# RWKV chunks: crossed halves, four array quarters for the second products, four heads as one group

## The reference, cut to what matters

```python
def step(state, inp):
    r_t, w_t, k_t, v_t, kk_t, a_t = inp
    sa = jnp.einsum('bhvk,bhk->bhv', state, -kk_t)
    state = (state * w_t[:, :, None, :] + sa[..., None] * (kk_t * a_t)[:, :, None, :]
             + v_t[..., None] * k_t[:, :, None, :])
    return state, jnp.einsum('bhvk,bhk->bhv', state, r_t)
```

## Time and profile before

| | |
|---|---|
| median of 3 runs | 3188.74 us (3184.62 to 3189.36) |
| profiled execution | 3188.14 us, span 3186.3 us |
| busy over the span | PE 3017.8 us (95%), PEld 2578.0 (81%), DVE 2129.0 (67%), ACT 1069.1 (34%), POOL 957.2 (30%) |
| mean granted TensorE clock | 0.985 of full |

### The profile page before, as it was taken

One profiled execution on the slowest core, in us unless ns is written; L12 is line 12 of the kernel. 1 busy time (PEld: TensorE's weight loads), 2 busy tenths in 40 slices (PEclk: granted clock), 3 DMA queues, 4 the chain that ended last, 5 costly groups with the idle time before them and its releaser, 6 DMA issues. The chain is left out here.

```text
span 3186.3 us, 44443 instructions
## 1 busy us (share of the span) xinstructions
PE 3017.8 (95%) x18182; PEld 2578.0 (81%) x18182; DVE 2129.0 (67%) x2634; ACT 1069.1 (34%) x1555; POOL 957.2 (30%) x656
## 2 busy tenths in 40 slices
PE   7999998999999999999998999898999999999997
PEld 7997888999888898887876786666777886888875
DVE  4535675445466646898836655777957757877798
ACT  2012433201133323322012221666415453344534
POOL 2320000333100013553322432111333443554575
PEclk9999999999999999999999999999999999999998
DMA  3111000111100002434242004321532543555543
GB/s 143 47 40 37 23 1 7 68 60 41 55 9 22 1 27 66 157 113 123 96 162 83 3 3 129 93 67 64 205 139 89 181 157 127 160 166 175 159 152 122
DMA packets 114818, 284.38 MB, mean 89 GB/s; under 512 B 15238, under 2 KB 20998, under 8 KB 114600
## 3 DMA queue, kind: packets, MB, share of 16 engines
q1 hardware_dynamic: 111304, 276.83, 26.9%
q10 hardware_dynamic: 3312, 4.72, 0.4%
HBM read 239.47 MB, written 41.44 MB: 88 GB/s over the span
## 5 line engine op out<-in xcount | busy, mean ns | idle before, releaser
L4082 PE MATMUL psum<-x,w_hi 128*128 128x512 f32 x2016 | 626.0, 392 | 8.3 <-DVE x L4053 3.2
L199 POOL CAST w_hi<-w_raw 128x1024 fp32r<-128x1024 f32 x98 | 109.0, 1112 | 1556.6 <-PE psum L212 953.6
L4082 PEld LDWEIGHTS psum<-x,w_hi 128*128 128x128 f32 x2016 | 378.5, 188 | 92.7 <-issue 7.0
L4082 PE MATMUL psum<-x,w_lo 128*128 128x512 f32 x1008 | 393.1, 390 | 0.0
L1061 PE MATMUL psum<-h,w_hi 128*128 128x512 f32 x1024 | 332.2, 406 | 18.8 <-PEq L126 8.5
L3967 POOL TENSOR_TENSOR w_lo<-w_sum,w_hi 128x512 fp32r<-128x512 f32 x180 | 250.6, 1399 | 330.9 <-ACT w_hi L3961 330.8
L203 POOL TENSOR_TENSOR w_lo<-w_raw,w_hi 128x1024 fp32r<-128x1024 f32 x98 | 258.7, 2640 | 14.9 <-DVE y L1876 7.2
L1061 PEld LDWEIGHTS psum<-h,w_hi 128*128 128x128 f32 x1024 | 190.8, 192 | 68.9 <-issue 21.6
L4082 PEld LDWEIGHTS psum<-x,w_lo 128*128 128x128 f32 x1008 | 189.8, 188 | 40.1
L212 PE MATMUL psum<-hn_hi,w_hi 128*128 128x348 f32 x864 | 188.9, 327 | 17.1 <-DVE hn_lo L409 15.7
L1061 PE MATMUL psum<-h,w_lo 128*128 128x512 f32 x512 | 203.1, 397 | 0.0
(11 more groups left out here) (503 smaller groups left out, 6557.3 us busy)
## 6 DMA issues: line engine op xcount, KB each, us to landing
w_raw<-in_w_mlp SPq DMA_DIRECT2D x169, 256.0 KB, 2.9
norm_factor<-in_w_mlp SPq DMA_DIRECT2D x87, 256.0 KB, 2.8
w_raw<-in_w_mlp SPq DMA_DIRECT2D x42, 512.0 KB, 3.6
w_raw<-in_w_in SPq DMA_DIRECT2D x36, 512.0 KB, 3.6
w_raw<-in_w_gates SPq DMA_DIRECT2D x32, 512.0 KB, 4.0
gates_kept<-gate_stage SPq DMA_DIRECT2D x64, 256.0 KB, 2.2
gates<-gates_kept SPq DMA_DIRECT2D x32, 512.0 KB, 3.3
w_raw<-in_w_out SPq DMA_DIRECT2D x24, 512.0 KB, 3.6
```

What stands on the lines that cost most here:

```text
L199: self.core.nc.gpsimd.tensor_copy(self.hi[:, g % 2], self.raw[:, g % 2]).then_inc(self.hi_done, 1)
L4082: last = self.core.nc.tensor.matmul(out, one[:, k, :], other[:, k, :], start=(group == 0 and k == 0 and part == 0), stop=(group == second ...
```

## The change

The two groups become one: each engine has one instruction, or one run of instructions, for all four heads at a level, and the semaphore counts are halved. XT is kept with its halves exchanged (what belongs to rows 0 to 63 lies on partitions 64 to 127, and the other way round; L2724 writes it so, L2754 reads it so). The first products write Y to the opposite half, bank 0. The second products XT^T Y go from a half to the opposite half (bank 0, columns 256 to 511), the products Y^T XT stay in their half (bank 1): together they use all four quarters. No matmul is added or removed. The core of the diff:

```diff
-    def pair_bank(g):
-        return psum[:, 2 + g, 0:256].rearrange("p (x h n) -> p x h n", x=2, h=2)
+    def pair_banks():
+        return psum[:, 0:2, 256:512].rearrange("p x (h n) -> p x h n", h=4)
 # ScalarE
-                        for g in range(2):
-                            act.wait_ge(y_done, 24 * c + 4 * n + 2 * g - 2)
-                            nc.scalar.activation(XY[rows, 2 * g:2 * g + 2, :].rearrange("p h n -> p (h n)"),
-                                                 psum[rows, g, 0:P], ACT.Copy).then_inc(y_saved, 1)
+                        act.wait_ge(y_done, 12 * c + 2 * n)
+                        nc.scalar.activation(XY[rows].rearrange("p h n -> p (h n)"), psum[rows, 0, 0:256],
+                                             ACT.Copy).then_inc(y_saved, 1)
 # VectorE
-                        for g in range(2):
-                            dve.wait_ge(xy_done, 24 * c + 4 * n + 2 * g - 2)
-                                both = inverses(c)[:, :, 2 * g:2 * g + 2, :]
-                                nc.vector.tensor_tensor(both, both, pair_bank(g), ALU.subtract).then_inc(inv_ready, 1)
+                        dve.wait_ge(xy_done, 12 * c + 2 * n)
+                            both = inverses(c)
+                            nc.vector.tensor_tensor(both, both, pair_banks(), ALU.subtract).then_inc(inv_ready, 1)
 # TensorE, first products
-                                pe.wait_ge(inv_ready, 12 * c + 2 * n + g - 3)
+                            pe.wait_ge(inv_ready, 6 * c + n - 1)
-                                for rows in halves_of:
-                                    last = nc.tensor.matmul(psum[rows, g, to], level(n)[rows, hd, :], X[rows, hd, :],
+                            for rows, other in crossed:
+                                last = nc.tensor.matmul(psum[other, 0, to], level(n)[rows, hd, :], X[rows, hd, :],
 # TensorE, second products
-                            pe.wait_ge(y_saved, 12 * c + 2 * n + g - 1)
+                        pe.wait_ge(y_saved, 6 * c + n)
-                                for rows in halves_of:
-                                    nc.tensor.matmul(to[rows, 0, e, :], XT[rows, hd, :], XY[rows, hd, :],
-                                for rows in halves_of:
-                                    last = nc.tensor.matmul(to[rows, 1, e, :], XY[rows, hd, :], XT[rows, hd, :],
+                            for rows, other in crossed:
+                                nc.tensor.matmul(to[other, 0, hd, :], XT[rows, hd, :], XY[rows, hd, :],
+                                last = nc.tensor.matmul(to[rows, 1, hd, :], XY[rows, hd, :], XT[rows, hd, :],
```

More of the change, by code:

```diff
@@ L2549, in rwkv_chunks @@
     halves_of = [slice(0, 64), slice(64, P)]
+    crossed = [(slice(0, 64), slice(64, P)), (slice(64, P), slice(0, 64))]
     gram = ybr[:, 6:8, :].rearrange("p a t -> p (a t)").rearrange("p (i h n) -> p i h n", i=4, h=4)
@@ L2636, in _ @@
                     if 0 <= c < count:
-                        for g in range(2):
-                            act.wait_ge(y_done, 24 * c + 4 * n + 2 * g - 2)
-                            rows = slice(0, P) if n < LEVELS - 1 else halves_of[1]
-                            nc.scalar.activation(XY[rows, 2 * g:2 * g + 2, :].rearrange("p h n -> p (h n)"),
-                                                 psum[rows, g, 0:P], ACT.Copy).then_inc(y_saved, 1)
+                        act.wait_ge(y_done, 12 * c + 2 * n)
+                        rows = slice(0, P) if n < LEVELS - 1 else halves_of[0]
+                        nc.scalar.activation(XY[rows].rearrange("p h n -> p (h n)"), psum[rows, 0, 0:256],
+                                             ACT.Copy).then_inc(y_saved, 1)
                     if c >= 1 and n == 1:
@@ L2697, in _ @@
                     if 0 <= c < count:
-                        for g in range(2):
-                            dve.wait_ge(xy_done, 24 * c + 4 * n + 2 * g - 2)
-                            if n < LEVELS - 1:
-                                both = inverses(c)[:, :, 2 * g:2 * g + 2, :]
-                                nc.vector.tensor_tensor(both, both, pair_bank(g), ALU.subtract).then_inc(inv_ready, 1)
-                            else:
-                                nc.vector.tensor_scalar(whole(c)[0:64, 2 * g:2 * g + 2, 64:P], pair_bank(g)[0:64, 0],
-                                                        -1.0, None, ALU.mult).then_inc(inv_ready, 1)
+                        dve.wait_ge(xy_done, 12 * c + 2 * n)
+                        if n < LEVELS - 1:
+                            both = inverses(c)
+                            nc.vector.tensor_tensor(both, both, pair_banks(), ALU.subtract).then_inc(inv_ready, 1)
+                        else:
+                            nc.vector.tensor_scalar(whole(c)[0:64, :, 64:P], pair_banks()[0:64, 1], -1.0, None,
+                                                    ALU.mult).then_inc(inv_ready, 1)
                     if c == 0 and n <= 4:
@@ L2722, in _ @@
                         dve.wait_ge(gram_saved, saved(f, 1))
-                        for rows in halves_of:
-                            link(nc.vector.tensor_tensor(XT[rows], AT(f)[rows, :, rows], half_mask(M_LEVEL, rows),
+                        for rows, other in crossed:
+                            link(nc.vector.tensor_tensor(XT[other], AT(f)[rows, :, rows], half_mask(M_LEVEL, rows),
                                                          ALU.mult))
@@ L2751, in widen @@
             def widen(c):
-                pool.wait_ge(inv_ready, 12 * c + 10)
-                for rows in halves_of:
-                    nc.gpsimd.tensor_copy(whole(c)[rows, :, rows], inverses(c)[rows, 1]).then_inc(whole_ready, 1)
+                pool.wait_ge(inv_ready, 6 * c + 5)
+                for rows, other in crossed:
+                    nc.gpsimd.tensor_copy(whole(c)[rows, :, rows], inverses(c)[other, 1]).then_inc(whole_ready, 1)
             pool.wait_ge(gates.core.weights.split_done, gates.g0 + gates.split_next + 1)
@@ L2760, in _ @@
                     if f:
-                        pool.wait_ge(y_done, 24 * (f - 1) + 4 * n)
+                        pool.wait_ge(y_done, 12 * (f - 1) + 2 * n)
                     for rows in halves_of:
@@ L2826, in end @@
                     pe.wait_ge(rhs_saved, c + 1)
-                    pe.wait_ge(inv_ready, 12 * c + 12)
+                    pe.wait_ge(inv_ready, 6 * c + 6)
                     pe.wait_ge(whole_ready, 2 * c + 2)
@@ L2873, in _ @@
                             pe.wait_ge(level_ready, 10 * c + 2 * n)
[L2874 to L2877, removed]
-                                pe.wait_ge(inv_ready, 12 * c + 2 * n + g - 3)
[L2879 to L2884, removed]
-                                for rows in halves_of:
-                                    last = nc.tensor.matmul(psum[rows, g, to], level(n)[rows, hd, :], X[rows, hd, :],
-                                                            start=True, stop=True)
-                                    if hd % 2:
-                                        last.then_inc(y_done, 1)
-                            if n == LEVELS - 1:
-                                last.then_inc(y_done, 2)
+                        if n == 1:
+                            pe.wait_ge(first_ready, 2 * c + 2)
+                        else:
+                            pe.wait_ge(inv_ready, 6 * c + n - 1)
+                        for hd in range(4):
+                            to = slice(64 * hd, 64 * hd + 64)
+                            if n == LEVELS - 1:
+                                last = nc.tensor.matmul(psum[0:64, 0, to], AT(c)[0:64, hd, 64:P], X[0:64, hd, :],
+                                                        start=True, stop=True)
+                                continue
+                            for rows, other in crossed:
+                                last = nc.tensor.matmul(psum[other, 0, to], level(n)[rows, hd, :], X[rows, hd, :],
+                                                        start=True, stop=True)
+                                if hd == 3:
+                                    last.then_inc(y_done, 1)
+                        if n == LEVELS - 1:
+                            last.then_inc(y_done, 2)
                     if c >= 1 and n <= 3:
@@ L2894, in _ @@
                     if 0 <= c < count:
-                        for g in range(2):
-                            pe.wait_ge(y_saved, 12 * c + 2 * n + g - 1)
[L2897 to L2906, removed]
-                                    nc.tensor.matmul(to[rows, 0, e, :], XT[rows, hd, :], XY[rows, hd, :],
-                                                     start=True, stop=True)
-                                for rows in halves_of:
-                                    last = nc.tensor.matmul(to[rows, 1, e, :], XY[rows, hd, :], XT[rows, hd, :],
-                                                            start=True, stop=True)
-                                    if e:
```

(21 more changed lines are left out.)

## The result

The changed kernel takes 3216.64 us (median of 4, 3214.6 to 3218.66), the kernel before 3189.01. The ratio is 1.009, 95% interval 1.0076 to 1.0105. I had said 3193, range 3188 to 3207.

What follows compares the result with a forecast made beforehand. Bound by TensorE's passes where neighbouring chunks fill waits, by the ring's latency elsewhere. Chunks 1 to 6 +2.2, chunk 7 +1.85, chunk 0 +0.5: +4.5 us on 3188.14 gives 3192.7, said as 3193, range 3188 to 3207.

Steps and rivals of the forecast that it cites:

- Four quarters at once, 0.46: Second products, 8 passes in each of four quarters: 0.46 us from first to last start, where it was 0.93.
- Rival 1: Quarters don't run four at a time; second products still take 0.93 us: 3208, or 3203 in part; chance 0.25.
- the estimate of 0.80 with a floor over all quarters together: Second products: 32 passes at about 25 ns start to start, 0.80 us, leaving a third of the 0.47 saving.
- The Trainium skill's rule on weight loads in one row group: Weight loads overlap running matmuls only in different row groups, so two quarters sharing a half would take turns.
- A: Latency from first products to second products through ScalarE's copy: 1.16 us, where it was 0.82.
- B: Latency from second products to next first products through VectorE: 1.59 us (1.50 into level 6), was 1.32 or 1.23.
- 0.69 and 0.38: Times in us of one 128x512 VectorE subtraction (0.69) and one ScalarE copy of 256 columns (0.38).
- Rival 3: VectorE ends last at levels 1 and 3, so shorter passes don't shorten them: near 3196; chance 0.07.
- VectorE tied to GpSimd at level 4, 2.68: Level 4: VectorE waits until GpSimd's instruction is over, 2.68 us from the level-4 first products' start.
- rival 2: L2740 and L2741 come to stand beside GpSimd's instructions, VectorE done 1.0 earlier: near 3188, no change; chance 0.08.
- TensorE's granted clock stays at its upper level: TensorE stays at 2.4 GHz: it held at 46% busy, and the new level 5 keeps it 51% busy.
- the first case: Four-way quarters with the ring as priced: 3193, own range 3190 to 3197; chance 0.60.

## Why the prediction was wrong, by its own steps

- *Four quarters at once, 0.46:* right, 0.48. Rival 1 is out, and so is the estimate of 0.80 with a floor over all quarters together: the passes of the four start 0.015 us apart on average. The Trainium skill's rule on weight loads in one row group (TensorE: Matmul & The Clock Gate, Part 3), weighed in the prediction, does not bind this form: two quarters with the same rows start within 0.01 us and keep to 0.06 a pass.
- *A = 1.16, B = 1.59 or 1.50; 0.69 and 0.38:* right within 0.04 nearly everywhere. A is 1.16 at level 4 (1812.85 to 1814.01) and 1.17 at level 5; B is 1.63 at level 2 (1806.99 to 1808.62) and 1.52 into level 6. At level 3 it is 1.70, since VectorE begins its subtraction 0.16 after the second products' end and not 0.07. Rival 3 is out with the subtraction at 0.69. At a full clock level 1 to level 6 last 3.38, 2.85, 4.23, 3.61, 2.69 and 2.39 (changed kernel with filled waits), against 3.36, 2.82, 4.13, 3.55, 2.66 and 2.40. The sum is 19.15 for 18.92, with the most, 0.10, at level 3. So the six chunks cost +3.6 by latency alone, not +2.2.
- *VectorE tied to GpSimd at level 4, 2.68:* nearly. L2740 (L2741 before) ends at 1815.58, 2.73 after the first products of level 4 (1812.85). It and L2739 keep their lengths, 0.94 and 0.84, so rival 2 is out.
- *"TensorE's granted clock stays at its upper level":* this is the step that failed. I took it from one stretch of chunk 0 in which PE was busy for 1.58 of 3.40 us at 1.00, and held the new level 5, busy for 51%, to be safer. The changed kernel's own line shows 2.05 busy of 3.83, a larger share than in rows 8, and the clock falls behind it. A stretch that I cut where it suited me was no evidence for another.
- *Its size.* Chunks 1 to 6 last 126.6 us together in the changed kernel (20.75, 20.73, 22.78, 20.84, 20.76, 20.76) and 6 x 19.15 = 114.9 with a held clock: the clock costs 11.7 us there. The end of the stage can be told apart too. The fence has the last second products and the last output copy (L2653) before, then changed, then changed with the waits of levels 4 to 6 filled, and for the last two a stretch with its clock (columns as in rows 2).

```profile
1904.62 0.91 PE L2903 MATMUL psum<-rw_mixed,xy 64*64 64x64 f32 x8
1909.89 0.38 ACT L2653 ACTIVATE branches<-psum 128x256 f32<-128x256 f32 x1 [1.66 <-PE psum L2849]
...
1925.63 1.11 PE L2899 MATMUL psum<-rw_mixed,xy 64*64 64x64 f32 x8 [0.47 <-ACT xy L2640]
1933.56 0.38 ACT L2653 ACTIVATE branches<-psum 128x256 f32<-128x256 f32 x1 [2.82 <-PE psum L2848]
1924.05:1933.56 9.51, 7.94 (x80) 7.00 (x80) 0.42 (x1) 1.15 (x4) 0.80 (x2) 0.52 0.00 0
...
1916.91 0.67 PE L2908 MATMUL psum<-rw_mixed,xy 64*64 64x64 f32 x8
1921.94 0.38 ACT L2653 ACTIVATE branches<-psum 128x256 f32<-128x256 f32 x1 [1.66 <-PE psum L2848]
1899.99:1921.94 21.95, 16.45 (x418) 13.26 (x416) 5.60 (x11) 4.21 (x11) 0.79 (x2) 1.00 0.01 2
```

Chunk 7, to the start of its last second products, lasts 15.4 before, 19.0 changed and 17.4 with a held clock (17.37 said): 2.0 of the 3.6 are latency, 1.6 are the clock. From there to the last output copy it is 4.6, 7.2 and 4.6: another 2.6 for the clock. Chunk 0 went from 19.7 to 21.8 (I had +0.5); its two causes aren't separated. Together: chunk 0 2.1, latency 3.6 + 2.0, clock 11.7 + 1.6 + 2.6, which is 23.6. The copy stands at 1909.9 before and at 1933.6 now, 23.7 later. The remaining 3.8 of the 27.5 us between the spans lie outside this stage, where no instruction was changed; their cause stays open.
- *The chances.* I gave 0.37 to slower, all of it for reasons that did not occur. Its working has a slip as well: a quarter of the first case's 0.60 is 0.15, not 0.10. Clock loss was not among the rivals, though the Trainium skill (TensorE: Matmul & The Clock Gate, HAM oscillation — how this bites in real kernels) names waits between bursts of matmuls as what brings it. The trace agrees: the falls come with levels 5 and 6, which have the waits and nothing to fill them. The waits are short ones: TensorE's longest in levels 5 and 6 of chunk 2 is 0.84 us, for VectorE.

## What to carry to other kernels

Price a new wait on TensorE twice: as latency, and as idle time that may cost the clock of what follows. When TensorE has less to do in a loop that gets no shorter, look for the longest run of steps with nothing to fill, and fill it: about 1 us of unused products in each chunk of 19 us (an estimate: 576 columns, two passes for each, at 0.058 us for 64 columns of a pass) took the changed kernel from 1.0090 to 1.0032. Splitting the heads into two groups was worth more than the four quarters: with a held clock 2.4 us a chunk (20.91 to 18.55) against 1.75 (20.91 to 19.15), or 1.3 with two groups (18.55 to 17.24). Both together give 17.24 a chunk and, filled, 0.9965.

## What the runs showed of the hardware

- Four 64x64 quarters run as four queues: four passes start within 0.02 us (1806.99 to 1807.01), and each quarter goes on every 0.06 us (0.10 after its first). Two quarters on the same rows have different moving data, and two row halves write the same partitions in different banks.
- The VectorE instructions with both inputs in SBUF that met a GpSimd instruction ended 0.27 to 0.29 us after that one's end: both by 0.29 before, 0.86 and 0.95 long, and by 0.28 and 0.27 in the changed kernel, 0.84 and 0.94 long. The 128x256 subtraction from PSUM kept 0.42 beside GpSimd's L2763 (L2702 at 1802.99, L2763 from 1801.93 to 1806.79).
- A fall of the clock lasts beyond the waits that stand ahead of it: level 1, in which TensorE is busy all the time (4.23 of 4.23 us at 0.77; 6.80 of 6.80 at 0.50 in the longer fall), pays for the waits of levels 5 and 6.
